# Gated one-hots of four tokens: one 512-wide comparison and one 512-wide product in place of four scalar operations

## What is computed

```python
s1 = jnp.einsum('nhd,kd->nhk', q[:, :, 0], sub_k1)      # 128 scores per head, first half of the key
s2 = jnp.einsum('nhd,kd->nhk', q[:, :, 1], sub_k2)
t1, i1 = lax.top_k(s1, 16)
t2, i2 = lax.top_k(s2, 16)
best, sel = lax.top_k(t1[..., :, None] + t2[..., None, :], 16)   # over the 256 pairs
idx = i1[...] * 128 + i2[...]                            # of those chosen by sel
gate = softmax(best)
u = take(u_tab, idx); h = gelu(u @ x)                    # per token and expert
out = sum over the 128 picks of gate * h * take(v_tab, idx)
```

## Time and profile before

| | us |
|---|---|
| median of 3 runs | 4941.49 (4933.53 to 4943.50) |
| the profiled execution, its own time | 4939.68 |
| its span, first to last instruction | 4937.8 |
| PE busy | 4690.6 (95%) |
| DVE busy | 2924.3 (59%) |
| POOL busy | 2248.9 (46%) |
| ACT busy | 1393.5 (28%) |

### The profile page before, as it was taken

One profiled execution on the slowest core, in us unless ns is written; L12 is line 12 of the kernel. 1 busy time (PEld: TensorE's weight loads), 2 busy tenths in 40 slices (PEclk: granted clock), 3 DMA queues, 4 the chain that ended last, 5 costly groups with the idle time before them and its releaser, 6 DMA issues. The chain is left out here.

```text
span 4937.8 us, 90870 instructions
## 1 busy us (share of the span) xinstructions
PE 4690.6 (95%) x35332; PEld 4498.4 (91%) x35332; DVE 2924.3 (59%) x4754; ACT 1393.5 (28%) x1798; POOL 2248.9 (46%) x865
## 2 busy tenths in 40 slices
PE   7999989999999898979999989999999999999997
PEld 6999888888888798979998989999999999999997
DVE  3333245555555432337786956656777777777777
ACT  3333322222222221122223333332323323322322
POOL 2222222221221143324443335556877877877876
PEclk8999999999999999989999999999999999999999
DMA  6999833333333277862334455546888888888884
GB/s 239 340 336 337 311 109 132 132 123 130 132 122 132 89 233 246 298 208 104 103 108 154 187 209 188 157 152 240 303 311 295 300 306 295 302 311 297 300 300 169
DMA packets 344271, 1078.94 MB, mean 219 GB/s; under 512 B 99456, under 2 KB 154112, under 8 KB 264960
## 3 DMA queue, kind: packets, MB, share of 16 engines
q1 hardware_dynamic: 292272, 784.66, 46.0%
q0 software_dynamic: 36864, 268.45, 14.5%
q10 hardware_dynamic: 14928, 22.84, 1.2%
HBM read 877.69 MB, written 198.14 MB: 218 GB/s over the span
## 5 line engine op out<-in xcount | busy, mean ns | idle before, releaser
L154 POOL TENSOR_TENSOR wlo<-raw,whi 128x2048 fp32r<-128x2048 f32 x174 | 803.5, 4618 | 2090.7 <-ACT whi L150 1792.9
L168 POOL TENSOR_TENSOR wlo<-raw,whi 128x1024 fp32r<-128x1024 f32 x424 | 1043.7, 2462 | 499.9 <-ACT whi L164 493.6
L164 ACT ACTIVATE whi<-raw 128x1024 fp32r<-128x1024 f32 x424 | 449.7, 1060 | 1009.9 <-PE psS L236 377.0
L236 PE MATMUL accs<-xh,whi 128*128 128x272 f32 x2624 | 577.7, 301 | 54.0 <-POOL wlo L154 26.5
L2234 DVE SCALAR_TENSOR_TENSOR Y<-R,HD,Y 128x2048 f32<-128x2048 f32 x127 | 440.0, 3465 | 235.0 <-DMA R<-in_v,IDX 230.6
L236 PE MATMUL accs<-xh,wlo 128*128 128x272 f32 x2624 | 547.0, 290 | 0.6 <-issue 0.6
L236 PE MATMUL accs<-xl,whi 128*128 128x272 f32 x2624 | 545.8, 290 | 0.0
L236 PE MATMUL accs<-hh,whi 128*128 128x272 f32 (+1 forms) x1696 | 464.7, 323 | 48.9 <-POOL wlo L154 23.4
L236 PEld LDWEIGHTS accs<-xh,whi 128*128 128x128 f32 x2624 | 415.5, 190 | 80.5 <-issue 36.1
L236 PE MATMUL psS<-hh,wlo 128*128 128x416 f32 x1344 | 474.8, 353 | 0.0
L236 PE MATMUL psS<-hh,whi 128*128 128x416 f32 x1344 | 471.8, 351 | 0.0
(11 more groups left out here) (398 smaller groups left out, 9593.4 us busy)
## 6 DMA issues: line engine op xcount, KB each, us to landing
raw<-in_u SPq DMA_DIRECT2D x128, 1024.0 KB, 5.0
raw<-in_v SPq DMA_DIRECT2D x128, 1024.0 KB, 5.7
raw<-in_w_in SPq DMA_DIRECT2D x82, 1024.0 KB, 8.1
at_UI<-in_u SPq DMA_DIRECT2D x64, 1024.0 KB, 9.1
u_d<-at_UO SPq DMA_DIRECT2D x256, 256.0 KB, 6.2
g_d<-STG SPq DMA_DIRECT2D x8, 3328.0 KB, 10.3
Ge<-g_d SPq DMA_DIRECT2D x64, 416.0 KB, 10.8
wo_UI<-in_u SPq DMA_DIRECT2D x24, 1024.0 KB, 8.5
```

What stands on the lines that cost most here:

```text
L154: pool.tensor_tensor(self.lo[:, c % 2, :], self.raw[:, c % 2, :], self.hi[:, c % 2, :].bitcast(F32), ALU.subtract).then_inc(self.split_don ...
L164: act.activation(self.half(self.hi, c, h), self.half(self.raw, c, h), ACT.Copy).then_inc(self.hi_done, 1)
L168: pool.tensor_tensor(self.half(self.lo, c, h), self.half(self.raw, c, h), self.half(self.hi, c, h).bitcast(F32), ALU.subtract).then_inc(se ...
L236: mm = pe.matmul(out, w(k), x(k, n), start=a, stop=z)
```

## The change

The four `tensor_scalar` of a quad go. In their place stand a 512-element comparison of `iota` with `IT[:, 0]` and, behind the comparison that was there already, a 512-element product in place with the gates `IT[:, 2]`. Since the product reads what the first comparison wrote, a new semaphore `gm_equal` is incremented by the first and waited for ahead of the product. `gm_onehot` is now incremented by the product. The matmuls and all other engines' programs are the same.

```diff
                     dve.wait_ge(S["gm_summed"], QUADS * i + turn(q))
-                    for j in range(4):
-                        tok = bass.ds(GB_T * i + 4 * q + j, 1)
-                        dve.tensor_scalar(ONE[:, SLOT[q], j, 0, :], iota[:, :], IT[:, 0, tok], IT[:, 2, tok], ALU.is_equal, ALU.mult)
-                    four = IT[:, 1, bass.ds(GB_T * i + 4 * q, 4)].unsqueeze(2).to_broadcast([P, 4, P])
-                    dve.tensor_tensor(ONE[:, SLOT[q], :, 1, :], iota[:, :].unsqueeze(1).to_broadcast([P, 4, P]), four,
-                                      ALU.is_equal).then_inc(S["gm_onehot"], 1)
+                    numbers = iota[:, :].unsqueeze(1).to_broadcast([P, 4, P])
+                    four = lambda a: IT[:, a, bass.ds(GB_T * i + 4 * q, 4)].unsqueeze(2).to_broadcast([P, 4, P])
+                    gated = ONE[:, SLOT[q], :, 0, :]
+                    dve.tensor_tensor(gated, numbers, four(0), ALU.is_equal).then_inc(S["gm_equal"], 1)
+                    dve.tensor_tensor(ONE[:, SLOT[q], :, 1, :], numbers, four(1), ALU.is_equal)
+                    dve.wait_ge(S["gm_equal"], QUADS * i + q + 1)
+                    dve.tensor_tensor(gated, gated, four(2), ALU.mult).then_inc(S["gm_onehot"], 1)
```

## The result

The change makes the kernel slower: 4985.55 us (median of 4 runs, 4983.35 to 4992.37) against 4942.23 before, a ratio of 1.0088 with a 95% interval of 1.0076 to 1.0100, so 43 us. The forecast was 4946.5, and its range ended at 4961. The profiled execution has a span of 4985.2 us.

What follows compares the result with a forecast made beforehand. PE and DVE were both nearly full; DVE would become the bound at 32.3 us a block instead of 31.34. DVE's 6.1 us delay, 4.4 reaching PE, plus 0.6 allowed gave 4941.5 + 5 = 4946.5 us, range 4932 to 4961.

Steps and rivals of the forecast that it cites:

- the standstills of 4.40 us: DVE's scalar operations before the change: one stands still under each POOL operation, two a block, 4.40 us each.
- The rival that wide operations don't stand still: Wide DVE operations immune to POOL: DVE needs 23.4 us a block, PE never waits, 4931 to 4932 us; chance 0.13.
- A quad at 1.80 us: DVE's three wide operations at 0.60 us each: 1.80 instead of 1.63 us a quad, 2.2 us more a block.
- the wait at 0: New semaphore wait ahead of DVE's product: hidden behind the second comparison, 0 us; without that cover 0.11 us a quad.
- Two SBUF inputs contend with POOL: DVE's wide operations aren't immune to POOL: a like comparison in line 1714 took 4844 ns against a median of 418.
- I take 4.43 for each POOL operation: DVE's standstill under each POOL operation after the change: 4.43 us, two a block, bounds 0 and 4.8.
- Rival 3: POOL waits for a run of wide DVE operations: 4942 to 4955 us, up to a microsecond a block for `wlo`; chance 0.10.
- DVE pauses after it is at most four quads ahead, 7.2 us of work: Argument limiting POOL's wait for DVE: DVE's lead over PE ends after four quads, 7.2 us of work.
- the slack: POOL's room for delay, taken from its wait for ACT ahead of its operations: 9.75 us to spare.
- whoever goes first [...] a block still needs the 32.3 us: DVE and POOL exclude each other, so their order leaves the block at 13 x 1.80 + 2 x 4.43 = 32.3 us.
- The forecast of 5 us on the stage: DVE ends 6.1 us later, 4.4 reach PE, 0.6 allowed for start and hand-over: +5 us; chance 0.50.
- slower: Whole kernel over 0.2% slower, above 4951.4 us: semaphore or read-back binding, POOL waiting, or the forecast's upper edge; chance 0.32.

## Why the prediction was wrong

- **Reading of the profile before: right.** Both engines nearly full, the standstills of 4.40 us, PE waiting 1.32 us a block for them. The rival that wide operations don't stand still would have gained 9 to 10 us; taking the contention away by PSUM or a small POOL operation gave 10.7 to 12.7 us, and a block of 29.77, which is that size.
- **A quad at 1.80 us and the wait at 0: right.** 2792.84 to 2794.64, and no idle time within a quad.
- **Two SBUF inputs contend with POOL: right.** 5073 ns for one product under the first POOL operation, and up to 5.09 us in the kernels with pauses.
- **"I take 4.43 for each POOL operation": this step failed.** The sum took it for granted that POOL gets in when it arrives, and so that DVE stands still 14 times. DVE stood still for a whole POOL operation once (the first), and in each later block POOL stood instead. DVE, forecast to be the bound and busy throughout, was busy for 24.80 of 37.50 us. The row that I relied on, 4844 ns in line 1714, was an arrival in the third operation behind a pause, a short one of 0.03 us of idle time, where POOL does get in.
- **The rival that had the mechanism was priced wrongly.** Rival 3 read the earlier trace rows as it had to be read: an arrival just as the seventh product of a run started (2583.15), and 1.3 us of waiting to its end. Its price went wrong in two sentences. "DVE pauses after it is at most four quads ahead, 7.2 us of work" forgot that PE frees slots meanwhile: DVE gains 2.3 - 1.8 = 0.5 us of lead a quad, so it doesn't fill its slots until PE stops, and PE stops for want of the very `wlo` that POOL can't make. Hence 13.9 us. And the slack was not 9.75 us, which is only how long POOL waits for ACT: `whi` was ready at 2784.25 and PE ran out of work at 2797.1, which less POOL's own 4.55 leaves 8.3 us. 13.9 - 8.3 is 5.6, PE's wait. And "whoever goes first [...] a block still needs the 32.3 us" holds for a shared resource that is never left idle. Here it was: while PE stands, DVE has full slots, and both POOL operations run one behind the other in that hole. With 0.10 for this case, and up to a microsecond a block for the `wlo` wait instead of 5.67, 4985 was outside.
- **The clock** was no term of the sum: 1.81 us of the 6.16 a block. A wait of 1.32 us had cost no clock, one of 5.67 did.
- The forecast of 5 us on the stage isn't far from what one operation in three reading two SBUF inputs does (255.0 against 250.1), nor from one pause in four quads (259.3). The rest of the sum fits a POOL that gets its turn; no run has the three operations as they are, without added pauses, and such a POOL.
- **A slip in the chances**: "slower" adds up to 0.22 + 0.03 + 0.05 = 0.30, not 0.32. It changes nothing above.

## What to carry to other kernels

Where VectorE and GpSimd both read SBUF, ask not only what each costs the other but whether GpSimd gets a turn: a steady run of VectorE operations with two SBUF inputs can shut it out until VectorE pauses, and if that pause depends on GpSimd's result through a third engine, the wait grows to that engine's whole slack and then stalls it. In such a stage one input in PSUM, once copied, frees both engines: here it took 12.7 us off the old form (`iota` alone is read from there) and 54 off the new (`iota` and the gates), and either then beat the kernel before. A long mean of an operation that nobody edited, on an engine with idle time, is the sign in the profile.

## What was not expected of the hardware

- GpSimd isn't passed over for good from the start: within the first four two-input VectorE operations behind a pause of 0.23 us or more it got in within 0.6 us, from the seventh on it didn't (23 passed it by in a row, 13.9 us at 0.60 each). One late arrival got in, two operations behind a break of only 0.08 us, so how short a pause suffices isn't settled. What changes between the fourth and the seventh isn't shown.
- VectorE operations of the same size differ in whether they let GpSimd in: scalar operations did (waits of 1.04 us at most beside them in the kernel with four scalar products), copies didn't (waits of up to 15.2 and 17.4 us).
- A comparison or product of 512 elements costs the same from PSUM and SBUF as from SBUF twice (678 to 684 ns); a scalar one of 128 goes from 336 to 400 ns.
- The Trainium skill (SBUF — State Buffer, who interferes with whom) says that an operation with at most one SBUF input, outside the two-port modes, doesn't contend; both PSUM kernels agree, with no standstill in 312 and 520 operations. Its sentence that the one who issues first gets the port and the other blocks doesn't cover the change: POOL was there ahead of 23 operations and went behind all of them; the measurement decides.
